# A two-block transformer stack at 256 tokens: the dense seams in another order, three weight units in places of their own, and five steps of one modulation product issued later

## The reference

```python
mod_l = jnp.split((silu_c @ ada_w[i] + ada_b[i])[:, None, :], 6, axis=-1)    # modulation vectors
y_l   = jnp.concatenate([o, fourier_groups(f, fourier_w)], axis=-1) @ w_out  # dense stage "out"
x = x + mod_l[2] * y_l                                                      # gated rows
x = x + mod_l[5] * swiglu(modulate(rmsnorm(x, ffn_norm_g[i]), mod_l[3], mod_l[4]),
                          ffn_w1[i], ffn_w3[i], ffn_w2[i])
def swiglu(h, w1, w3, w2):
    return (jax.nn.silu(h @ w1) * (h @ w3)) @ w2
```

## Time and profile before

| | us |
|---|---|
| three timed runs | 967.84, 969.5, 969.53 (median 969.5) |
| the profiled execution | 967.11 |
| its span, first to last instruction | 965.4 |
| PE busy | 906.9 (94%) |
| DVE busy | 738.4 (76%) |
| ACT busy | 468.7 (49%) |
| POOL busy | 134.3 (14%) |

### The profile page before, as it was taken

How to read it: one execution, slowest core, us unless ns; L and a number is a source line. 1 busy time by engine, 2 the same in 40 slices (tenths; PEclk the granted TensorE clock), 3 DMA queues, 4 the chain that set the end, 5 groups by cost and what they waited for, 6 DMA issues and landing times.

```text
span 965.4 us, 12492 instructions
## 1 busy us (share of the span) xinstructions
PE 906.9 (94%) x4323; PEld 713.5 (74%) x4323; DVE 738.4 (76%) x1074; ACT 468.7 (49%) x782; POOL 134.3 (14%) x204
## 2 busy tenths in 40 slices
PE   3899999989999999899988999999979998999996
PEld 1687766767888888677566788888867776878875
DVE  1598689888768677889678877678698888976674
ACT  2462358554344443553185434434435876645651
POOL 0001130405001300030003210021001110001000
PEclk8999999999999999999999999999989999999999
DMA  9988743459988889547624798898857346695001
...
DMA packets 121239, 229.09 MB, mean 237 GB/s; under 512 B 8667, under 2 KB 64701, under 8 KB 121195
## 3 DMA queue, kind: packets, MB, share of 16 engines
...
q10 hardware_dynamic: 2170, 0.64, 0.3%
...
HBM read 227.43 MB, written 1.08 MB: 237 GB/s over the span
## 4 chain that ended last, share of the span: by engine, by line
PE 73%; DVE 12%; issue 6%; ACT 5%; DMA 2%; POOL 1%; SPq 0%; ACTq 0%; DVEq 0%; POOLq 0%
PE bank L2089 21%; PE bank L2091 20%; PE bank L2090 20%; PE bank L2669 1%; DVE w_lo L1262 1%; DVE x L1344 1%; DVE job_sum L1279 1%; DMA x<-x_dram 1%; DVE w_lo L1375 1%; DVE tmp L1343 1%; DMA w_land<-ev_w_in_dram 1%; ACT w_hi L697 1%; PE bank L2510 1%; PE bank L2170 1%; PE bank L2128 1%
## 5 line engine op out<-in xcount | busy, mean ns | idle before, releaser
L2089 PE MATMUL bank<-w_hi,xT_hi 128*128 128x512 f32 x800 | 323.9, 405 | 13.3 <-DVE xT_lo L1388 6.7
L2091 PE MATMUL bank<-w_hi,xT_lo 128*128 128x512 f32 x800 | 315.1, 394 | 0.0
L2090 PE MATMUL bank<-w_lo,xT_hi 128*128 128x512 f32 x800 | 314.2, 393 | 0.0
L1262 DVE TENSOR_TENSOR w_lo<-w_land,w_hi 128x2048 fp32r<-128x2048 f32 x109 | 250.1, 2298 | 83.3 <-ACT w_hi L697 83.1
L697 ACT ACTIVATE w_hi<-w_land 128x2048 fp32r<-128x2048 f32 x109 | 208.4, 1916 | 112.8 <-PE bank L2091 104.9
L2089 PEld LDWEIGHTS bank<-w_hi,xT_hi 128*128 128x128 f32 x800 | 151.9, 190 | 55.4 <-issue 18.5
L2091 PEld LDWEIGHTS bank<-w_hi,xT_lo 128*128 128x128 f32 x800 | 151.5, 189 | 33.0
L2090 PEld LDWEIGHTS bank<-w_lo,xT_hi 128*128 128x128 f32 x800 | 152.3, 190 | 28.7
L1279 DVE SCALAR_TENSOR_TENSOR job_sum<-a_land,silu_c,job_sum 128x1024 f32<-128x1024 f32 x126 | 164.1, 1303 | 5.5 <-DMA a_land<-mod_w_dram 1.7
L2089 PE MATMUL bank<-w_hi,hT_hi 128*128 128x512 f32 x176 | 69.9, 397 | 2.8 <-DVE hT_lo L1704 2.8
L2091 PE MATMUL bank<-w_hi,hT_lo 128*128 128x512 f32 x176 | 68.7, 390 | 0.0
...
## 6 DMA issues: line engine op xcount, KB each, us to landing
...
```

What stands on the lines that cost most here:

```text
L1262: dve.tensor_tensor(w_lo[u % N_SPLIT][:, :], w_land[n % N_LAND][:, :], w_hi[u % N_SPLIT][:, :].bitcast(F32), ALU.subtract).then_inc(s_lo, 1)
L2089: pe.matmul(dst, hi, whi, start=start, stop=False)
L2090: pe.matmul(dst, hi, wlo, start=False, stop=False)
L2091: return pe.matmul(dst, lo, whi, start=False, stop=stop)
```

## The change

1. **Places aside.** The first units of `ffn0`, `ffn1` and `kv` get places of their own inside the large scratch area, so their splits wait for no unit. The unit after each of them takes the place that would have been theirs and is free one unit earlier (`freed`); later units keep their terms.
2. **Order of a dense seam on DVE** (`dense_residual`). Before: the splits of units 2 and 3, residuals (0,0) and (0,1), the split of the next stage's first unit, residual (1,0), mean, `xn`, both halves of the unit after. Now: the split of unit 2, residual (0,0), the splits of unit 3 and of the next stage's first unit, the first half of the unit after, residual (1,0), then residual (0,1) with the mean between its two instructions, `xn`, the second half. ACT squares tile 0 in both column halves first, and makes its copies of all these units ahead of the squares.
3. **Job 3.** Three of its steps stood ahead of or in the `out` seam, on DVE, and two right behind the operand of `ffn0`. Now one of these five stands behind that operand and four behind the first gated rows `hidden(0)`, around the split of unit `ffn0 + 3`. Its last transfer is issued on POOL behind the norm of `ffn0`. PE's `job_sums(3)` moves from ahead of the first transposes of hidden rows into the first pair of `ffn0`, which is written out ahead of the loop; ACT's copy of that row moves behind the split of `ffn0 + 3`.
4. **POOL.** The zero rows come ahead of the loads of job 4. The tap and bias transfers of the later convolution, and the bias rows in `ffn1`, wait for the first unit of their feed-forward stage to be used up. The last transfer of job 4 goes ahead of `gate_rows(3)`.

The core of the diff:

```diff
+ASIDE = {BASE["ffn0"]: 0, BASE["ffn1"]: 1, BASE["kv"]: 2}
+def _places():
+    order, places = list(range(N_SPLIT)), []
+    for u in range(UNITS):
+        if u in ASIDE:
+            places.append(N_SPLIT + ASIDE[u])
+            a, b = u % N_SPLIT, (u + 1) % N_SPLIT
+            order[a], order[b] = order[b], order[a]
+        else:
+            places.append(order[u % N_SPLIT])
+    return places
+def freed(u):
+    return u - N_SPLIT if u - 1 in ASIDE else u - N_SPLIT + 1
...
+        w_hi += [place(f"w_hi_aside{i}", [P, UNIT], BIG, R32) for i in range(3)]
+        w_lo += [place(f"w_lo_aside{i}", [P, UNIT], BIG + o * KB, R32) for i, o in enumerate((31, 17, 29,))]
...  (POOL)
-            load_job(3, ada[0], 5 * D, range(2, 4))
+            load_job(3, ada[0], 5 * D, (2,))
...
             pow_tiles("n_ffn0")
+            zero_ffn()
+            load_job(3, ada[0], 5 * D, (3,))
             load_job(4, ada[1], 0, range(2))
-            zero_ffn()
 
             pool.wait_ge(*seen("lo", "sub", HEADS))
             pool.wait_ge(sem("four_y"), 1)
+            pool.wait_ge(s_used, BASE["ffn0"] + 1)
...
             load_job(4, ada[1], 0, (2,))
+            load_job(4, ada[1], 0, (3,))
             gate_rows(3)
-            load_job(4, ada[1], 0, (3,))
...
+            pool.wait_ge(s_used, BASE["ffn1"] + 1)
             load_bias(9, ada_b[1:2, 5 * D:6 * D])
...  (ACT)
-                if u >= N_SPLIT:
-                    act.wait_ge(s_used, at(u - N_SPLIT + 1, i, 6))
-                act.activation(w_hi[u % N_SPLIT][:, :], ...
+                if u >= N_SPLIT and u not in ASIDE:
+                    act.wait_ge(s_used, at(freed(u), i, 6))
+                act.activation(w_hi[PLACE[u]][:, :], ...
...
             head_out(len(ITS) - 1)
+            split_hi(BASE["out"] + 2)
             full_hi("sub", o_full, xT_hi, range(4, HEADS), 4)
...
-                if stage not in ("pw2", "att_out"):
+                if stage == "rg_out":
                     split_hi(BASE[stage] + 2)
                 split_hi(BASE[stage] + 3)
                 split_hi(BASE[stage] + 4)
-                half_squares(after, residual_steps, (0, 1, 2))
+                if stage != "att_out":
+                    split_halves(BASE[stage] + 5)
+                half_squares(after, residual_steps, (0, 1, 2), tiles_first=True)
                 if stage == "att_out":
-                    half_squares(after, residual_steps, (3,))
-                else:
-                    split_halves(BASE[stage] + 5)
+                    half_squares(after, residual_steps, (3,), tiles_first=True)
...
                 silu(0, base)
+                split_hi(base + 3)
+                hidden_hi(0)
                 if layer == 0:
                     job_copy(first_job - 1)
-                split_hi(base + 3)
-                hidden_hi(0)
...  (DVE)
+            def residual_late(c, t, b, wait, between):
...
+                dve.wait_ge(*wait)
+                dve.tensor_tensor(part, bank[b][:, :], gate[:, cols], ALU.mult).then_inc(sem("dve_chain"), 1)
+                between()
+                dve.wait_ge(sem("dve_chain"), done)
                 dve.tensor_tensor(x[:, t, cols], x[:, t, cols], part, ALU.add).then_inc(sem("xres"), 1)
...
-            job_units(3, (1,))
+            job_units(3, (1,), None, (0,))
...
                 residual(0, 0, 0, seen("part", stage, 1))
-                residual(0, 1, 1, (s_used, BASE[stage] + 2))
-                split_lo(BASE[stage] + 4)
+                split_lo(base + 3)
+                split_lo(base + 4)
+                unit = base + 5
+                if unit < UNITS:
+                    split_lo_half(unit, 0, half_ready(unit))
                 residual(1, 0, 2, seen("part", stage, 2))
-                tile_mean(after, 0, 3)
+                residual_late(0, 1, 1, (s_used, base + 2), lambda: tile_mean(after, 0, 2))
...
                 if layer == 0:
+                    job_units(3, (1,), None, (1,))
+                hidden(0)
+                if layer == 0:
+                    job_units(3, (2,), None, (0,))
+                split_lo(base + 3)
+                if layer == 0:
+                    job_units(3, (2,), None, (1,))
                     job_units(3, (3,))
-                hidden(0)
-                split_lo(base + 3)
                 hidden_lo(0)
                 job_units(first_job, range(2) if layer == 0 else range(2, 4))
...  (PE)
                 first_chunk(f"n_ffn{layer}", base, AFTER_DENSE, True)
-                if layer == 0:
-                    job_sums(first_job - 1)
                 turn_hidden(0)
...
+                if layer == 0:
+                    pair(0, first_job, None, first_job - 1)
+                    done = 1
+                with pe.Fori(0, loops - done) as i:
+                    pair(done, first_job + done, i)
```

76 lines of the change are left out of this document (40 added, 36 removed).

## The result

The changed kernel takes 971.99 us (median of 8 runs, 970.17 to 973.26) beside 967.84 us for the kernel before in the same comparison: ratio 1.0041, 95% interval 1.0028 to 1.0055. It is slower by 4 us, 0.4%, with an interval clear of 1. Forecast was +0.3 us, no change that a measurement could tell. The time itself lies inside the stated range of 963.5 to 973. The same kernel, run once more as a base for the experiments, gave 971.49 us and a ratio of 1.0032 [1.0013, 1.0051].

A forecast was written before the change was run, and what follows sets the result against it. PE was taken to bound the kernel, busy 906.9 of 965.4 us. +3.5 at `ffn0`'s opening (including the 4.4 gained before it), -2.3 at `pw2`, -0.9 at `rg_out` gave +0.3, on the mean 968.5: 968.8 us, range 963.5 to 973.

The forecast's parts named there:

- Before's own fall at 220 cost nothing: Opening of `ffn0`, kernel before: its lower clock near 220 cost 0 us, since PE would have waited for the same split.
- The `out` seam: Attention output's seam: DVE's operand starts at 197.6 instead of 202.01, 4.4 us earlier; transposes of tile 1 come at 204.1.
- `pw2` and `rg_out`: The two later seams: the operand comes 2.3 us earlier at `pw2` and 0.9 us earlier at `rg_out`.
- The wait of 0.7 for `w_lo` at `rg_out`: In `rg_out`, the split of unit `rg_out + 3` is ready at 805.0, PE wants it at 804.26: a new wait.
- Rival C: Seams give nothing, as the late squares of quarter (0,1) hold up the mean: sum +2.4, 970.9 us; chance 0.10.
- The wait at the first product on hidden rows: Opening of `ffn0`: PE waits 7.2 us for the split of `ffn0 + 4`, ready at 234.3, ending 2.1 us behind before.
- POOL's add: Opening of `ffn0`: the add in `gate_rows(3)` falls on the decisive split, costing 0.4 us, left in the range.
- Rival B: Opening of `ffn0`: longer stall, job 4's second transfer queues behind its first; at 10.9 us landing +3.9, 972.4 us; chance 0.22.
- The clock behind the wait: Opening of `ffn0`: after the pause PE resumes at the lower clock, taken as 1.4 us lost.
- Rival A: Opening of `ffn0`: job 4's second transfer lands 5.2 to 6 us after issue; sum -3.2 to -4.4, 965 us; chance 0.22.

The follow-up runs named there:

- e10: e2 with the `out` seam put back into its order of before on DVE and ACT, leaving the late seams reordered: 964.8 us, ratio 0.9964.
- e2: The changed kernel with job 3 put back as in the kernel before, its sums and copy too; seam order and places aside stay: 962.9 us.
- e8: The changed kernel run once more, unaltered, as a base for the experiments: 971.49 us, ratio 1.0032.
- e3: The kernel before with job 3's four steps, transfers, sums and copy moved as in the change, seams as before: 977.1 us.
- e4: The changed kernel with POOL's tap and bias transfers of the convolution issued behind the last two loads of job 4: 969.3 us.
- e7: The changed kernel with 28 unused products on PE filling the wait before the first product on hidden rows of `ffn0`: 970.1 us, ratio 1.0018.
- e11: The changed kernel with DVE's first `ffn0` pair reordered, POOL's convolution transfers later, and job 5's first two loads ahead of the gate: 970.5 us, ratio 1.0014.
- e5: The changed kernel with DVE's first `ffn0` pair written out, splits and hidden-row products ahead of job 4's steps that wait for data: 969.1 us.
- e12: e2 run a second time, beside e11: 961.2 us, the same ratio as its first run.

## Why the prediction was wrong

The mechanism, the places and the wait were as forecast; the sum, +0.3 against a measured +3.1 to +4.0 by the two ratios, is 2.8 to 3.7 us too low. The step that failed most plainly is a term put at nothing: "Before's own fall at 220 cost nothing". Term by term:

- The `out` seam. Operand forecast at 197.6, measured 197.87; 4.4 us forecast at `up`, 4.2 measured. Right, but for 0.5 us at the transposes of tile 1 (forecast 204.1, measured 204.62), which the job 3 steps behind them inherit.
- `pw2` and `rg_out`. Forecast 2.3 and 0.9, measured 2.3 and 0.95 in the trace and 3.5 for both in e10. The wait of 0.7 for `w_lo` at `rg_out` is 0.53. The transposes of tile 0 were to follow without a wait in `out` and `pw2` and wait 0.39 and 0.51 us. Right in the main. Rival C is out by e2.
- The wait at the first product on hidden rows. Forecast 7.2 us, measured 7.4; its end was forecast 2.1 us behind before and came 2.9 behind. The second transfer of job 4 was asked for at 221.64 instead of 221.1 and took 8.6 us instead of 8.3, and the split took 2.5 instead of 2.24 us beside POOL's add, which the prediction had left in the range. By 0.7 us too small here. In e8, counted from each trace's own `diff`, it is 0.3. Rival B, which had the sign of the result, needed a landing of 9.5 us, and its transfer took 8.6 and 7.8.
- **"Before's own fall at 220 cost nothing", the step that failed.** It was argued that PE would otherwise have waited for the split. By the rows of before the split was ready at 230.9, and e10 has the product at 230.44 with no wait: the fall had cost 1.4 us of 232.27 at least, 1.9 by e10, and the new stall was compared with a start that was already late. Whoever takes that fall out of before gets 3.5 for the stall's end instead of 2.1, and a sum of 1.7 instead of 0.3. This counts in full if most executions of before have no fall there, as the other three traces of this order have none.
- **The clock behind the wait, perhaps mis-sized.** 1.4 us were taken, nearer to the 1.0 us of the window with 0.80 than to the 2.8 of the other. Behind 7.4 us 13 matmuls took 0.43 instead of 0.23 us: 2.6 us, and e3 (7.2 us, 13 matmuls) is the same. e4 (5.9 us, 7 matmuls) and e8 (6.6 us, 7 matmuls) lost half of that, and e7 puts it at 1.4 to 2.2 over many runs. So the term was up to 1.2 us too small, or right.

Together this is 0.3 to 0.7 for the end of the wait, 1.4 to 1.9 for the fall of before and 0 to 1.2 for the clock behind the wait: 1.7 to 3.8 us, which covers those 2.8 to 3.7. The table says the same. From e10, which has the opening of before at full clock, the stretch grew by 5.8 us (e8) and 7.3 us (the first trace), and `pw2` and `rg_out` gave 3.2 back: +2.6 to +4.1 in all. The move of job 3 is the whole loss: the difference between e2 (-5.9) and the changed kernel is 9 to 10 us, more than the 8.0 that e3 shows for the move alone.

How much of this is clock is not settled. The runs of the changed kernel have a mean granted clock of 0.978, those of before and e2 0.983, and within the runs of one kernel 0.01 of clock goes with 3 to 8 us. That would be some 1.5 to 4 us, and one stall explains only a part of it: by an estimate, 5.3 us at 0.50 (the slow matmuls behind the wait) take 0.003 off the mean of the whole span. In the traces, slow matmuls near 411 and 428 us (in each kernel's own time) occur in seven of the ten traces that have job 3 in the opening, in e11 at the second place only, and in none of the four without. The stretch from the last chunk of `ffn0` to the last wait before `pw2` takes 99.8 to 100.0 us in those seven and 96.6 to 96.7 in e4, e5, e8, e12 and before. But the fast order isn't free of falls: in the trace of e2 the clock was at the lower level for 10 us further on, and that stretch took 101.3. Windows of e2:

```profile
478.00:483.00 5.00, 5.00 (x12) 3.40 (x11) 2.76 (x4) 0.63 (x2) 0.72 (x1) 0.50 0.23 38
483.00:488.00 5.00, 5.00 (x12) 3.30 (x11) 4.75 (x8) 4.22 (x9) 0.00 (x0) 0.50 0.46 188
```

So the later falls are not shown to be an effect of the change. Why a wait at 230 should bring a fall at 411 no run here shows.

The chances were at fault with the sum. Rival A took 0.22 for a transfer that lands sooner, although the only row at the place said 8.3, while every unpriced thing pointed to slower: POOL's add, a longer fall, two transfers close together. They had been left in the range and out of the sum.
